# Out-product of a two-layer trunk kernel: the group norm's root before the gate copies, the last two head turns inside the sixth tile, two turns before the meeting, and the second low half first

## What is computed

```
y = head_layer_norm(y, RW_GN_EPS) * gn_g[d] + gn_b[d]            # RWKV branch, per direction d
out = out + (y + bonus) * g                                      # g = sigmoid(gd) @ rw_g_up
mixed = concat([o_rw, o_gla, o_diff], -1)                        # 256 + 256 + 512 columns
m = mixed @ w_out                                                # the out-product, 1024 x 1024
x = layer_norm(ALPHA * x + g2 * m)
```

## Time and profile before

| | us |
|---|---|
| median of 3 runs | 2077.01 |
| lowest and highest of them | 2076.71, 2080.94 |
| the profiled execution's own time | 2068.53 |
| its span, first to last instruction | 2066.4 |

### The profile page before, as it was taken

The page is one execution under the profiler, slowest core; times in us unless marked ns, Lnnn a source line. Parts: engine busy times, 40 slices in busy tenths (PEclk is TensorE's granted clock), DMA queues, the critical chain, the costliest instruction groups (busy, mean ns, idle before and its releaser), DMA issues. The chain is left out here.

```text
span 2066.4 us, 37089 instructions
## 1 busy us (share of the span) xinstructions
PE 1923.4 (93%) x16090; PEld 1727.6 (84%) x16090; DVE 1040.4 (50%) x1601; ACT 716.4 (35%) x1182; POOL 31.9 (2%) x61
## 2 busy tenths in 40 slices
PE   7999999998799889999999999999986888999996
PEld 5899998986569769999979999989754876899996
DVE  2344335655575675443374333466456757633336
ACT  3322224435452343222252222353366224422221
POOL 0000000000000001000000000000000000000000
PEclk9999999999889999999999999999996899999998
DMA  7733335332760134333344333413341002433320
GB/s 319 307 125 122 122 122 224 125 120 85 318 253 5 46 143 180 127 122 122 122 164 148 133 125 122 143 62 122 126 193 72 3 12 100 162 127 133 124 102 31
DMA packets 40398, 274.52 MB, mean 133 GB/s; under 512 B 4602, under 2 KB 6538, under 8 KB 8272
## 3 DMA queue, kind: packets, MB, share of 16 engines
q1 hardware_dynamic: 35280, 255.34, 34.3%
q0 software_dynamic: 2384, 13.75, 1.7%
q10 hardware_dynamic: 2608, 3.56, 0.5%
HBM read 269.22 MB, written 3.41 MB: 132 GB/s over the span
## 5 line engine op out<-in xcount | busy, mean ns | idle before, releaser
L2114 DVE TENSOR_TENSOR ring_r<-ring,arena_r 128x1024 fp32r<-128x1024 f32 x328 | 387.9, 1222 | 707.6 <-ACT arena_r L1618 707.1
L894 PE MATMUL bank<-arena_r 128*128 128x384 f32 (+3 forms) x2056 | 701.4, 341 | 22.7 <-DVE ring_r L2114 13.6
L897 PE MATMUL bank<-arena_r 128*128 128x384 f32 (+2 forms) x1816 | 603.5, 332 | 0.0
L898 PE MATMUL bank<-arena_r,ring_r 128*128 128x384 f32 (+2 forms) x1816 | 602.2, 332 | 0.0
L894 PEld LDWEIGHTS bank<-arena_r 128*128 128x128 f32 x2056 | 390.9, 190 | 45.7 <-issue 21.3
L1618 ACT ACTIVATE arena_r<-ring 128x1024 fp32r<-128x1024 f32 x340 | 340.5, 1052 | 150.2 <-PE bank L898 146.8
L897 PEld LDWEIGHTS bank<-arena_r 128*128 128x128 f32 x1816 | 342.1, 188 | 3.5
L898 PEld LDWEIGHTS bank<-arena_r,ring_r 128*128 128x128 f32 x1816 | 342.4, 189 | 0.0
L959 PE MATMUL bank<-arena_r 128*128 128x512 f32 x1128 | 310.9, 393 | 0.3 <-issue 0.3
L1749 ACT ACTIVATE arena<-bank 128x384 f32<-128x384 f32 x88 | 43.3, 492 | 735.0 <-PE bank L898 735.0
L959 PEld LDWEIGHTS bank<-arena_r 128*128 128x128 f32 x1128 | 210.7, 188 | 42.2 <-issue 1.2
(11 more groups left out here) (287 smaller groups left out, 1822.9 us busy)
## 6 DMA issues: line engine op xcount, KB each, us to landing
ring<-weights SPq DMA_DIRECT2D x242, 1024.0 KB, 4.9
lnrow<-ln_in POOLq DMA_DIRECT2D x6, 1024.0 KB, 6.4
const<-consts POOLq DMA_DIRECT2D x1, 2211.0 KB, 10.1
x<-x_in ACTq DMA_DIRECT2D x1, 1536.0 KB, 13.8
y_out<-x SPq DMA_DIRECT2D x3, 512.0 KB, 2.6
rows<-row_in POOLq DMA_DIRECT2D x2, 704.0 KB, 10.5
par<-par_in POOLq DMA_DIRECT2D x2, 662.5 KB, 7.6
wad<-w_ad POOLq DMA_DIRECT2D x2, 256.0 KB, 9.6
```

What stands on the lines that cost most here:

```text
L894: mm = pe.matmul(out, w_h, h_h, start=start, stop=False, skip_group_check=True)
L897: pe.matmul(out, w_h, h_l, start=False, stop=False, skip_group_check=True)
L898: return pe.matmul(out, w_l, h_h, start=False, stop=stop, skip_group_check=True)
L2114: ve.tensor_tensor(low_unit((l, name), u) if out is None else out, raw, place.bitcast(F32), ALU.subtract).then_inc(w_ready, 1)
```

## The change

The turns get their own banks and become functions outside `mix_out`. Turns 0 and 1, and ACT's copies and roundings of both, move ahead of the meeting. Turns 6 and 7 move from behind tile 5 into it, behind its first token group. ACT's root of the group norm moves ahead of the first two gate copies. ACT's copies of turns 6 and 7 stay in their place. In `turn_x`, DVE's low half of unit 1 now stands ahead of the third group's statistics also for j = 2.

```diff
+MIX_BANK = (1, 2, 1, 0, 1, 0, 1, 0)
 # PE
+                    def mix_turn(n):
+                        k = OUT_ORDER[n]
+                        if n >= 2:
+                            pe.wait_ge(mix_read, n - 1)
+                        for g in range(GROUPS):
+                            mm = pe.transpose(ps[MIX_BANK[n]][:, g * P:g * P + P], mixed[:, g, k * P:k * P + P], ident)
+                        mm.then_inc(mix_turned, 1)
...
-                        for n in range(4):
-                            turn(n)
+                        for n in range(2, 4):
+                            mix_turn(n)
...
                         for n in range(KT - 2):
                             for g in range(GROUPS):
                                 mm = tile(n, g)
+                                if n == KT - 3 and g == 0:
+                                    pe.wait_ge(heads_out, 1)
+                                    pe.wait_ge(gates_out, 3)
+                                    mix_turn(6)
+                                    mix_turn(7)
                             mm.then_inc(out_mm, 1)
...
-                        pe.wait_ge(heads_out, 1)
-                        pe.wait_ge(gates_out, 3)
-                        turn(6)
-                        turn(7)
...
                     rwkv_units()
+                    mix_turn(0)
+                    mix_turn(1)
                     meet()
                     mix_out()
 # ACT
+                    def mix_pair(n):
+                        mix_turn(n)
+                        mix_turn(n + 1)
+                        mix_high(n)
+                        mix_high(n + 1)
...
-                        for n in range(0, 4, 2):
-                            turn(n)
-                            turn(n + 1)
-                            high(n)
-                            high(n + 1)
+                        mix_pair(2)
                         weight(1)
...
-                        high(4)
-                        high(5)
+                        mix_high(4)
+                        mix_high(5)
+                        sc.wait_ge(rw_var, 1)
+                        sc.activation(gn_var, gn_var, ACT.Sqrt).then_inc(rw_std, 1)
                         gates(0)
                         gates(1)
-                        sc.wait_ge(rw_var, 1)
-                        sc.activation(gn_var, gn_var, ACT.Sqrt).then_inc(rw_std, 1)
                         weight(3)
...
                     rwkv_units()
+                    mix_pair(0)
                     meet()
 # DVE, turn_x
-                        if j != 2:
-                            weight(1)
+                        weight(1)
                         rest(n, 2)
                         scale(n, 2)
                         if j != 1:
-                            for u in range(1 if j == 2 else 2, 4):
+                            for u in range(2, 4):
                                 weight(u)
```

More of the change, by code:

```diff
@@ L1520, in rwkv_units @@
                         outer((4, 0), 2)
-                    def mix_out():
[L1523 to L1529, removed]
+                    def mix_turn(n):
[5 more added lines that the diff above has]
+                        mm.then_inc(mix_turned, 1)
+                    def mix_out():
                         def gates(pair):
@@ L1557, in mix_out @@
                                 mm = tile(n, g)
+                                if n == KT - 3 and g == 0:
[3 more added lines that the diff above has]
+                                    mix_turn(7)
                             mm.then_inc(out_mm, 1)
                             if n == 0:
-                                turn(4)
-                                turn(5)
+                                mix_turn(4)
+                                mix_turn(5)
                             elif n == 1:
@@ L2023, in rwkv_units, with mix_turn, mix_high @@
                         round_unit("out", 0, out_w_hi[0])
+                    def mix_turn(n):
+                        sc.wait_ge(mix_turned, n + 1)
+                        k = OUT_ORDER[n]
+                        sc.activation(mixT[:, k, :], ps[MIX_BANK[n]][:, 0:TOK], ACT.Copy,
+                                      scale=prm("gla_gc") if k in (2, 3) else 1.0).then_inc(mix_read, 1)
+                    def mix_high(n):
+                        k = OUT_ORDER[n]
+                        sc.wait_ge(mix_read, n + 1)
+                        sc.activation(mixT_hi[:, k, :], mixT[:, k, :], ACT.Copy).then_inc(mix_rounded, 1)
+                    def mix_pair(n):
[3 more added lines that the diff above has]
+                        mix_high(n + 1)
                     def rwkv_gates():
@@ L2028, in mix_out @@
                     def mix_out():
[L2029 to L2033, removed]
                         def gates(pair):
@@ L2038, in gates @@
                             sc.activation(out, ps[pair % 2][:, :], ACT.Copy).then_inc(gates_out, 1)
[L2040 to L2043, removed]
                         def weight(m):
@@ L2070, in mix_out @@
                         weight(5)
+                        mix_turn(6)
+                        mix_turn(7)
                         for n in range(6, KT):
-                            turn(n)
-                        for n in range(6, KT):
-                            high(n)
+                            mix_high(n)
                             weight(n)
```

## The result

| | before | after |
|---|---|---|
| median, us (runs) | 2077.01 (7) | 2059.48 (7) |
| lowest and highest | 2074.35, 2081.15 | 2053.01, 2068.77 |
| the profiled execution's own time | 2068.53 | 2068.77 |

The ratio is 0.9917, with a 95% interval of 0.9891 to 0.9943: 17.5 us less, for a forecast of 16.2. So the two spans can't be subtracted. What can be compared is a stretch between two landmarks: from the start of the last product of `outer` to the first product of the feed-forward's third token group. It holds all edits, once in each layer: 697.88 to 775.45 before and 707.13 to 773.34 after in layer 0, and likewise in layer 1.

What follows compares the result with a forecast made beforehand. TensorE, busy 93%, was taken as the bound, so only its waits and slow clock count: 2.0 + 3.0 + 4.6 + 3.2 + 1.5 + 2.4 - 0.5 = 16.2 us, from 2077.0 to 2060.8; range 2051 to 2070.

Steps and rivals of the forecast that it cites:

- Turns 0 and 1 ahead of the meeting, 2.0: Between `outer` and tile 0: ScalarE ends the meeting later, but only turns 2 and 3 follow; 2.0 us over both layers.
- The clock at the start, -0.5: At tile 0: layer 0 may have fewer slow products, layer 1 more; -0.5 us, bounds -4.5 and +2.
- The root, 3.0: Group norm: the earlier root removes TensorE's waits at tiles 3, 4 and 5, 1.5 us a layer; 3.0 us together.
- The heads, 4.6: Turns 6 and 7 within tile 5: copies hidden, 1.1 us pause left; 2.3 us per layer, 4.6 together.
- the clock behind their pause, 2.4: Layer 1, after the idle 3.25 us: 12 products at the lower clock level become fast, 2.4 us.
- Without the root's move it would be late by 2 us: Inside tile 5: with the root in its old place, the heads' sum would come 2 us late for TensorE's turns.
- Rival (b): Root comes no earlier: waits at tiles 3 to 5 stay, heads delay tile 5; gain 9.2, 2067.8 us, chance 0.09.
- The second low half, 3.2 and 1.5: Feed-forward's start: the 2.07 us wait goes, third group's products start sooner; 3.2 us in layer 0, 1.5 in layer 1.
- nothing later takes it back: In the feed-forwards behind, TensorE's at 93% busy: no later code was expected to lose the gain.
- Wrong if the clock is at 0.50 through tiles that ran at 1.00: Listed sign against the forecast: tiles formerly at full clock running at 0.50, which is 1.2 of 2.4 GHz.

Runs made afterwards that it cites:

- root late: The changed kernel with ScalarE's root of the group norm back behind the first two gate copies: 2068.82 us, ratio to before 0.9957.
- heads late: The changed kernel with turns 6 and 7 back behind tile 5: 2072.35 us, ratio to before 0.9972.
- low half late: The changed kernel with unit 1's low half back behind the third group's statistics: 2062.64 us, ratio to before 0.9927.
- turns late: The changed kernel with turns 0 and 1 and ScalarE's copies back behind the meeting: 2070.08 us, ratio to before 0.9966.
- root alone: The kernel before with only the root's move ahead of the gate copies: 2076.86 us, ratio to before 0.9990.
- heads alone: The kernel before with only turns 6 and 7 moved within tile 5: 2071.89 us, ratio to before 0.9951.
- units last: The changed kernel with VectorE's low halves of units 2 and 3 behind the third group's modulation and low halves: 2053.11 us, ratio to before 0.9883.
- five in the pause: The changed kernel with five unread products in the pause ahead of the third group's first products: 2054.43 us, ratio to before 0.9890.
- six: The changed kernel with six unread products of the identity between turn 1 and the meeting: 2062.74 us, ratio to before 0.9906.
- three products: The changed kernel with three unread products of the identity between turn 1 and the meeting: 2060.09 us, ratio to before 0.9920.
- three and five: The changed kernel with three unread products ahead of the meeting and five ahead of the third group's products: 2056.03 us, ratio to before 0.9897.
- the three edits together: The changed kernel with three unread products at the meeting, units 2 and 3's low halves later, third group's turns before its selection: 2055.11 us, ratio 0.9882.

## Why the prediction was right, point by point

- **Turns 0 and 1 ahead of the meeting, 2.0:** right in its mechanism, low in size: 2.82 here, and 3.0 for both layers on average over the kernel after and the three experiments that put another part of it back (root, heads and low half late; 4.12 us to tile 0) against the four with the old order (before, turns late, root and heads alone; 5.60). ScalarE does end the meeting: the turns behind it begin 3.0 us after the end of `outer`, for the 3.1 worked out. The mis-sized term is what follows: half of 3.12 us, 1.35, for turns 2 and 3. The 3.12 had been measured at the lower clock (0.50 in both layers); at the upper level, as in layer 0, tile 0 follows the meeting after 711.12 - 710.44 = 0.68 us.
- **The clock at the start, -0.5:** 0.04 here. Over the same eight stretches on each side `outer` to tile 1 fell from 11.89 to 9.83 us, 2.06 a layer, of which the start is 1.48. So the clock gives some 0.6 a layer: a wrong sign. Tile 0 was slow in 7 of 8 stretches with the old order, in 3 of 12 with the early turns (the same kernels with "units last" and "five in the pause"), and in none of 8 with unread products. The Trainium skill (TensorE: Matmul & The Clock Gate, What's actually happening) says that the number of slow matmuls of one kernel changes from run to run; these counts agree, though they also move with what is placed ahead.
- **The root, 3.0:** 4.1, at the upper bound of 4.0. The waits at tiles 3, 4 and 5 went, and a little more: 2.0 a layer, where the three waits of 1.5 had been taken. The term was mis-sized because a wait row is shorter than the stop: products in a stream start 0.23 us apart, but each is recorded as lasting 0.39, and the wait is counted from that end. So in layer 1 the step from the last product of tile 4 to the first of tile 5 fell from 0.66 to 0.24 us, 0.42 for a wait listed as 0.27.
- **The heads, 4.6, and the clock behind their pause, 2.4:** 7.34 for 7.0. The pause left is 0.45 us ahead of tile 6 and 0.31 ahead of tile 7, not 1.1 ahead of tile 6: the hand-overs between engines, taken at 0.1 to 0.2 us, are below 0.05 in these rows (740.33 + 1.23 to 741.60), and unit 6's rounding waits for tile 4 and can lie inside tile 5 (739.23); only unit 7's waits for tile 5.
- **"Without the root's move it would be late by 2 us":** wrong, as "root late" and "heads alone" show. The working took the start's 1.25 and the 1.5 of the waits off TensorE's time and not off VectorE's, though VectorE starts earlier by the first as well, and the second isn't gained without the root. On equal terms TensorE arrives at 736.67 - 1.25 - 2.8 = 732.6 and the heads at 733.16 - 1.25 = 731.9, 0.7 us to spare: the 0.70 that "root late" measured. Rival (b)'s price holds that error: 7.0 us lost without the root, for the 4.3 that the stretches of "root late" show.
- **The second low half, 3.2 and 1.5:** 5.04 for 4.7 in the stretch, and VectorE's list ends last, as worked out, though it idles 2.25 us in it, for ScalarE's rounding. But the prediction's "nothing later takes it back" failed. With the new order the clock fell right behind the third group's start in 6 of 12 stretches with the pause of 1.39 us (after, root, heads and turns late, six and three products). In layer 1 each fall cost 4.8 us of tail (295.2 for 290.4 in all three). At one fall in two stretches that is 4.8 in an execution of two layers too, about the whole gain of this part. With the pause filled or shortened there was none in 8 stretches ("five", "three and five", the three edits together, "units last"), so the pause probably has a part in it (6 of 12 against 0 of 8 comes by chance about once in forty). But behind the same pause at the third place there was none in 9 either, so something else, perhaps what stands ahead of it, has a part as well; what that is stays open. With the old order the clock fell too, one pause earlier: at the wait of 2.07 us in 5 of 8 stretches (before's layer 0, both of "low half late" and of "root alone"), at 1.5 us each, and then not again behind the third group. On average over these 8 the way from the feed-forward's first products to the third group's took 14.4 us, for 11.65: 5.5 us for both layers, less the 4.8 of the falls. "Low half late", 3.2 us slower with intervals that overlap, fits such a small net gain.
- **"Wrong if the clock is at 0.50 through tiles that ran at 1.00":** that did happen, in tile 0 of layer 1 and behind the third group. It was too little to turn the result, and the terms that came out larger, by 3.1 us in all, made up for part of it: 19.3 of stretch less 4.8 is 14.5 in this execution, for 16.2. That the median came as close as 17.5 is partly luck.

What stays open: the medians of "turns late" and "heads late" lie 10.6 and 12.9 us above after's, while the stretches show 3.2 and 4.5. The intervals of the ratios allow some 6 us less on either, and one profiled execution shows only one draw of the clock. The mean granted clock of every execution tells part of the rest. Over 179 executions of all the kernels, the time grows by 1.1 us for each 0.001 that the clock is lower, with a scatter of 2.4 us around that. "Turns late" and "heads late" ran at 0.957 and 0.956 on average, after at 0.960; at the same clock they lie 5.7 and 6.5 us above after's, each give or take 2.4, and "units last" 2.2 below it. So about half of the excess goes with the clock, and the rest agrees with the stretches as far as this error allows. Why these two kernels ran at a lower clock isn't shown.

## What to carry to other kernels

A reordering that removes a wait can lengthen the next one by half a microsecond, and if the clock falls behind that, more is lost than the half: look at each pause of TensorE that is left and at the clock in the ten microseconds behind it, not only at the sum of the waits. Look, too, for a second place with the same pause before calling the pause the cause. When a shift of the start is carried through a chain, take it off both sides of every meeting point, and take from each side only what the case in hand has gained. Where equal code scatters by 9 us with the clock, cut the trace at landmarks around the change; two whole spans of 2066.4 us said "no difference" here about a kernel that is 0.8% faster.

## What the hardware showed beyond that

The fall behind the third group doesn't come with the pause, but later, when TensorE is working again without a gap. In layer 1 of the kernel after, the products restart at 1771.23 at 0.11 us from start to start, and lengthen from 1773.71 on (TensorE's timeline):

```profile
1771.23 0.30 PE L895 MATMUL bank<-arena_r 128*128 128x128 f32 x1 [1.40 <-DVE arena_r L2170]
1771.36 0.28 PE L898 MATMUL bank<-arena_r 128*128 128x128 f32 x1
...
1773.60 0.28 PE L895 MATMUL bank<-arena_r 128*128 128x128 f32 x1
1773.71 0.39 PE L898 MATMUL bank<-arena_r 128*128 128x128 f32 x1
1773.89 0.42 PE L899 MATMUL bank<-arena_r,ring_r 128*128 128x128 f32 x1
```

Products that nobody reads may pay: five in a pause that is there anyway cost nothing (11.65 us from the feed-forward's first products to the third group's, without them and with them), and the clock stayed up in all four stretches in which they stood there, which would come by chance once in sixteen at six falls in twelve; six ahead of a meeting cost 1.5 us where the clock was already low. And ScalarE's table load doesn't wait with its root: it ran from 719.19 to 720.47, ahead of the variance at 720.80, so that the root itself took 0.22 us once its input was there.
